# Low-rank log-decay from stacked parts; output projection 2 begins with tokens 0-127; the last gate's sums in two idle stretches

## The reference

```python
mod = jnp.einsum('bd,de->be', silu_c, w_ada[l]) + b_ada[l]
shift1, scale1, gate1, shift2, scale2, gate2 = jnp.split(mod, 6, axis=-1)
h = modulate(rms_norm_2(x, norm1_w[l]), shift1, scale1)
proj = jnp.einsum('btd,de->bte', h, w_in[l])
q, k, v, r, a_lr, su, sv, g_a, g_b = jnp.split(proj, IN_SPLITS, axis=-1)
z = jnp.einsum('btr,rk->btk', a_lr, w_alpha_up[l]) + b_alpha[l]      # rank 16
log_a = jax.nn.log_sigmoid(z.astype(jnp.float32)) / GLA_TAU
o = gla_chunked(q, k, v, log_a)                                     # per head
o_gla = rms_norm_2(o, gla_norm_w[l]) * jax.nn.silu(r)
o_sgu = spatial_gating(gelu(su), gelu(sv), sgu_w[l], sgu_b[l], sgu_ln_w[l], sgu_ln_b[l])
merged = jax.nn.sigmoid(g_a) * o_gla + jax.nn.sigmoid(g_b) * o_sgu
y = jnp.einsum('bte,ed->btd', merged, w_out[l])
x = x + gate1[:, None, :] * y
h2 = modulate(rms_norm_2(x, norm2_w[l]), shift2, scale2)
y2 = peer(h2, peer_w_q[l], peer_keys1[l], peer_keys2[l], peer_down[l], peer_up[l])
x = x + gate2[:, None, :] * y2
```

## Time and profile before

| | us |
|---|---|
| median of 3 runs | 1362.02 |
| lowest, highest | 1361.2, 1363.53 |
| the profiled execution's own time | 1364.04 |
| its span | 1361.8 |
| TensorE busy | 1345.7 |
| GpSimd busy | 1052.1 |
| VectorE busy | 764.7 |
| ScalarE busy | 714.2 |

### The profile page before, as it was taken

One profiled execution on the slowest core, in us unless ns is written; L12 is line 12 of the kernel. 1 busy time (PEld: TensorE's weight loads), 2 busy tenths in 40 slices (PEclk: granted clock), 3 DMA queues, 4 the chain that ended last, 5 costly groups with the idle time before them and its releaser, 6 DMA issues.

```text
span 1361.8 us, 27395 instructions
## 1 busy us (share of the span) xinstructions
PE 1345.7 (99%) x9123; PEld 1176.2 (86%) x9123; DVE 764.7 (56%) x1627; ACT 714.2 (52%) x1145; POOL 1052.1 (77%) x466
## 2 busy tenths in 40 slices
PE   9999999999999999999999999999999999999997
PEld 8798999998788877899999988888888888888886
DVE  4765433336224346289980488888887787411113
ACT  6464655555365445345556544444455555565654
POOL 6665788886787866968888877777777777788885
PEclk9999999998999999999999999999999999999999
DMA  8555677773655455745555545545555454565552
GB/s 311 182 182 189 241 279 283 282 255 110 233 176 183 159 205 211 260 136 180 184 185 185 185 156 170 166 157 169 170 171 170 161 167 164 207 224 191 194 191 102
DMA packets 73056, 263.08 MB, mean 193 GB/s; under 512 B 8224, under 2 KB 9120, under 8 KB 72624
## 3 DMA queue, kind: packets, MB, share of 16 engines
q1 hardware_dynamic: 73008, 262.46, 56.4%
HBM read 259.81 MB, written 2.62 MB: 193 GB/s over the span
## 4 chain that ended last, share of the span: by engine, by line
PE 95%; DVE 3%; ACT 1%; DMA 1%; issue 0%; POOL 0%; SPq 0%; POOLq 0%; DVEq 0%; ACTq 0%
PE bank L1008 15%; PE bank L1010 15%; PE bank L1009 15%; PE bank L989 11%; PE bank L966 8%; PE bank L967 8%; PE bank L968 8%; PE bank L990 5%; PE bank L1486 3%; PE bank L993 2%; PE bank L992 1%; PE bank L1152 1%; PE bank L1468 1%; PE bank L1184 1%; DVE bank L1614 0%; DMA raw<-stream 0%
## 5 line engine op out<-in xcount | busy, mean ns | idle before, releaser
L453 POOL TENSOR_TENSOR wlo<-raw,whi 128x1024 fp32r<-128x1024 f32 x432 | 1037.5, 2413 | 282.5 <-ACT whi L532 281.1
L532 ACT ACTIVATE whi<-raw 128x1024 fp32r<-128x1024 f32 x432 | 456.0, 1057 | 326.9 <-PE bank L1010 257.0
L1008 PE MATMUL bank<-whi,xhl 128*128 128x512 f32 x792 | 314.0, 397 | 1.8 <-DVE xhl L1567 1.6
L1010 PE MATMUL bank<-whi,xhl 128*128 128x512 f32 x792 | 308.9, 390 | 0.0
L1009 PE MATMUL bank<-wlo,xhl 128*128 128x512 f32 x792 | 308.2, 389 | 0.0
L966 PE MATMUL bank<-xhl,whi 128*128 128x256 f32 x896 | 255.0, 285 | 1.9 <-DVE xhl L1572 1.1
L967 PE MATMUL bank<-xhl,whi 128*128 128x256 f32 x896 | 253.5, 283 | 0.0
L968 PE MATMUL bank<-xhl,wlo 128*128 128x256 f32 x896 | 253.4, 283 | 0.0
L989 PE MATMUL bank<-xhl,whi 128*128 128x512 f32 x616 | 222.1, 399 | 0.7 <-DVE xhl L1567 0.7
L1008 PEld LDWEIGHTS bank<-whi,xhl 128*128 128x128 f32 x792 | 148.8, 188 | 34.3 <-DVE xhl L1567 1.9
L966 PEld LDWEIGHTS bank<-xhl,whi 128*128 128x128 f32 x896 | 171.7, 192 | 5.6 <-issue 1.4
(11 more groups left out here) (327 smaller groups left out, 1504.3 us busy)
## 6 DMA issues: line engine op xcount, KB each, us to landing
raw<-stream SPq DMA_DIRECT2D x432, 512.0 KB, 3.3
arena<-ada SPq DMA_DIRECT2D x48, 512.0 KB, 4.7
arena<-rows SPq DMA_DIRECT2D x5, 512.0 KB, 7.6
xs<-x SPq DMA_DIRECT2D x2, 512.0 KB, 6.0
arena<-rows SPq DMA_DIRECT2D x1, 1024.0 KB, 5.9
x_spill<-xs SPq DMA_DIRECT2D x1, 1024.0 KB, 6.6
xs<-x_spill SPq DMA_DIRECT2D x1, 1024.0 KB, 5.5
arena<-hgmask SPq DMA_DIRECT2D x1, 512.0 KB, 8.0
```

The lines of the kernel that those rows point to most:

```text
L453: nc.gpsimd.tensor_tensor(wlo[:, slot, :], raw[:, slot, :], whi[:, slot, :].bitcast(F32), ALU.subtract).then_inc(lo_done, 1)
L532: nc.scalar.activation(whi[:, slot, :], raw[:, slot, :], ACT.Copy).then_inc(hi_done, 1)
L1008: nc.tensor.matmul(bank[b][:, :], ah[:, ts], whi[:, slot, cs], start=start, stop=False)
L1010: last = nc.tensor.matmul(bank[b][:, :], al[:, ts], whi[:, slot, cs], start=False, stop=final)
```

## The change

It has five parts.

1. `ada_columns` of groups 2 to 5 moves 64 columns of ones instead of one; 63 of the 64 results are overwritten or not used.
2. The low-rank product down reads `xhl` directly, in fp32r: ScalarE rounds the 16 weight columns, VectorE puts their rest in 16 more columns beside them, and 8 matmuls with these 32 columns move `xh` and `xl` of a k block together (512 columns). The copies of the modulated rows to the arena (L1970) go, and the product moves from ahead of the group `m_sv` to ahead of its third tile.
3. The low-rank product up stacks three parts on 96 partitions: the weight matrix is sent six times over, and partitions 0-31 hold its upper part, 32-63 the rest, 64-95 the upper part again, against the upper, upper and lower part of the 32 rows from below. Four fp32r matmuls.
4. The transposes of the merged rows go bank by bank, a bank holding four k blocks of 128 tokens. Bank 0's stand ahead of the last product of `m_gb`. Output projection 2 takes k blocks 0 to 2 for tokens 0-127 first, then for tokens 128-255, then k blocks 3 to 5 for all, and the last two bank by bank as before.
5. The last gate's eight tiles have a buffer each, in a dead buffer and in three that are free by then; SP issues them in bursts of 4, 2 and 2 during `m_v` and `m_r`, VectorE sums six of them behind the spatial gating and two behind the second product of the r rows.

The diff, cut (lines of waits and buffers that the text has told are left out):

```diff
@@ buffers
-        mv, mr, mga, mgb, msu, msv = (take(2048, TT, D) for _ in range(6))
+        mv, mr, mga = (take(2048, TT, D) for _ in range(3))
+        spare = take(2048)
+        msu, msv = (take(2048, TT, D) for _ in range(2))
...
+        late_ada = [b_[:, j * 1024:(j + 1) * 1024]
+                    for b_ in (spare, rw.rearrange("p a b -> p (a b)"), qk.rearrange("p a b -> p (a b)"),
+                               msv.rearrange("p a b -> p (a b)")) for j in range(2)]
@@ SyncE
+            sp.wait_ge(S("rw_copied"), 4)
+            for j in range(4):
+                late_ada_tile(j)
+            for n in range(T_IN2_M + 24, T_WOUT2 + 8):
                 tile(n % R, n * P, n - R + 1)
-            for n in range(ADA_FIRST + R, ADA_FIRST + R + 4):
-                ada_tile(n)
+                if n == T_IN2_M + 31:
+                    sp.wait_ge(S("g_qk"), 4)
+                    late_ada_tile(4)
+                    late_ada_tile(5)
+                if n == T_IN2_M + 35:
+                    sp.wait_ge(S("sgu_mm"), 4)
+                    late_ada_tile(6)
+                    late_ada_tile(7)
@@ ScalarE
+            upper_of(T_IN2_F + R + 3, T_IN2_M + 3)
             act.wait_ge(S("consts2_in"), 96)
+            nc.scalar.activation(wal_hl[:, :, 0:16], wal, ACT.Copy)\
+                .then_inc(S("rank_hi"), 1)
+            nc.scalar.activation(wup_hl, wupt, ACT.Copy).then_inc(S("rank_hi"), 1)
...
+            merged_upper(0)
             upper_of(T_WOUT2 + 2, T_WOUT2 + 3)
             act.wait_ge(tile_used, T_IN2_M + 48)
             nc.scalar.activation(bank[3][:, :], bank[3][:, :], ACT.Sigmoid).then_inc(S("gb_out"), 1)
-            upper("merged_T", first=4)
-            upper_of(T_WOUT2 + 3, T_WQ)
+            merged_upper(1)
+            upper_of(T_WOUT2 + 3, T_WOUT2 + 4)
+            merged_upper(2)
+            merged_upper(3)
+            upper_of(T_WOUT2 + 4, T_WQ)
@@ TensorE
-            def ada_columns(g):
+            def ada_columns(g, n=1):
...
-                    last = nc.tensor.matmul(bank[7][:, 4 * g + j:4 * g + j + 1], ada_sum(g)[:, j * P:(j + 1) * P], one,
-                                            start=True, stop=True)
+                    last = nc.tensor.matmul(bank[7][:, 4 * g + j:4 * g + j + n], ada_sum(g)[:, j * P:(j + 1) * P],
+                                            one.to_broadcast([P, n]), start=True, stop=True)
...
-                ada_columns(g)
+                ada_columns(g, 64)
...
+            def low_rank(n):
+
+                if n != 2:
+                    return
+                pe.wait_ge(S("gate1_done"), 2)
+                pe.wait_ge(S("rank_lo"), 1)
+                for k in range(KC):
+                    last = nc.tensor.matmul(bank[6][0:32, :], wal_hl[:, k, :],
+                                            xhl[:, :, k, :], start=(k == 0), stop=(k == KC - 1))
+                last.then_inc(S("alr"), 1)
+
+            m_group(T_IN2_M, "m_sv", before=low_rank)
...
+                    if tt and h == 2:
+                        pe.wait_ge(ada_used, N_ADA)
...
+            def merged_turn_first(b, k):
+                if (b, k) == (3, KC - 1):
+                    merged_turn(0)
...
+            m_group_by_banks(T_IN2_M + 40, "m_gb", 2, ahead=merged_turn_first)
+            merged_turn(1)
+            wout2_part(0, (0, 1))
+            wout2_part(1, (0, 1))
+            merged_turn(2)
+            wout2_part(2, (0, 1))
+            merged_turn(3)
+            for k in range(3):
+                wout2_part(k, (2, 3))
+            for k in range(3, KC - 2):
+                wout2_part(k, range(4))
+            for b in range(4):
+                for k in range(KC - 2, KC):
+                    wout2_part(k, (b,))
@@ VectorE
-            for b in range(4):
-                nc.vector.tensor_copy(xg[:, 2 * b:2 * b + 2, :],
-                                      bank[IN2_BANKS[b]][:, :].rearrange("p (a t) -> p a t", a=2))\
-                    .then_inc(S("xg_out"), 1)
...
+            ttt(wal_hl[:, :, 16:32], wal, wal_hl[:, :, 0:16].bitcast(F32), ALU.subtract).then_inc(S("rank_lo"), 1)
+            ttt(wup_hl[32:64, :], wupt[32:64, :], wup_hl[32:64, :].bitcast(F32), ALU.subtract).then_inc(S("rank_lo"), 1)
             v.wait_ge(S("alr"), 1)
-            nc.vector.tensor_copy(alT, bank[6][0:16, 0:T]).then_inc(S("alr_out"), 1)
+            al = bank[7][0:32, 0:T]
+            own(nc.vector.tensor_reduce(al, bank[6][0:32, :].rearrange("p (a t) -> p t a", a=2), AX.X, ALU.add))
...
+            ttt(al_hl[64:96, :], al, al_hl[0:32, :].bitcast(F32), ALU.subtract)\
+                .then_inc(S("alr_out"), 1)
...
+            v.wait_ge(S("sgu_done"), 4)
+            for n in range(ADA_FIRST, ADA_FIRST + 6):
+                ada_tile(n)
             read_out("m_r", T_IN2_M + 32, mr, "r_out")
...
+            for n in range(ADA_FIRST + 6, N_ADA):
+                ada_tile(n)
             v.wait_ge(S("ga_out"), 4)
...
+            merge(0)
+            merge(1)
+            merged_lower(0)
+            merge(2)
+            merged_lower(1)
+            merge(3)
+            merged_lower(2)
+            merged_lower(3)
```

More of the change, by code:

```diff
@@ L1378, in _ @@
                     ada_row(9)
[L1380 to L1387 removed]
+            def low_rank(n):
[8 more added lines that the diff above has]
+            m_group(T_IN2_M, "m_sv", before=low_rank)
+            pe.wait_ge(S("rank_lo"), 2)
             pe.wait_ge(S("alr_out"), 1)
             for h in range(4):
[L1390 to L1391 removed]
+                last = nc.tensor.matmul(bank[6 + h // 2][:, (h % 2) * T:(h % 2 + 1) * T], wup_hl[:, h * P:(h + 1) * P],
+                                        al_hl, start=True, stop=True)
             last.then_inc(S("z_mm"), 1)
@@ L1432, in _, with merged_turn, wout2_part @@
             last.then_inc(S("gla_o"), 1)
-            m_group_by_banks(T_IN2_M + 40, "m_gb", 2)
-            turn_of("merged_T", go, "merged_out", 0, range(4))
-            turn_of("merged_T", go, "merged_out", 1, (0, 1))
-            def go_turn_rest(k):
-                if k == 1:
-                    turn_of("merged_T", go, "merged_out", 1, (2, 3))
-            m_group_by_banks(T_WOUT2, "wout2", 2, "merged", before=go_turn_rest)
+            def merged_turn(b):
+                pe.wait_ge(S("merged_out"), b + 1)
+                if b == 0:
+                    name, n = acc_freed("merged_T", b)
+                    pe.wait_ge(S(name), n)
+                for j in range(4):
+                    k = 4 * (b % 2) + j
+                    last = nc.tensor.transpose(bank[4 + b][:, j * P:(j + 1) * P], go[:, b // 2, k * P:(k + 1) * P],
+                                               ident[:, :])
+                last.then_inc(acc_ready, 1)
+            def merged_turn_first(b, k):
+                if (b, k) == (3, KC - 1):
+                    merged_turn(0)
+            def wout2_part(k, banks):
+                pe.wait_ge(S("turned_lo"), turn("merged", 4, 2 * (banks[-1] // 2) + k // 4 + 1))
+                m_tile((T_WOUT2 + k) % R, T_WOUT2 + k + 1, xh[:, k, :], xl[:, k, :], "wout2" if k == 0 else None,
+                       final=(k == KC - 1), banks=banks, used=banks[-1] == 3)
+            m_group_by_banks(T_IN2_M + 40, "m_gb", 2, ahead=merged_turn_first)
[12 more added lines that the diff above has]
+                    wout2_part(k, (b,))
             for g in (10, 11):
@@ L1600, in ada_tile @@
                 g, m = n // 4, n % 4
[L1601 to L1603 removed]
+                acc_ = bank[6 if R <= n < ADA_FIRST else 7][:, :]
+                if n < ADA_FIRST:
+                    w_ = adar[:, n % R, :]
+                    v.wait_ge(ada_full[n % R], 16 * (n // R + 1))
+                else:
+                    w_ = late_ada[n - ADA_FIRST]
+                    v.wait_ge(ada_full[(n - ADA_FIRST) // 2], 16 * (ADA_FIRST // R) + 32)
                 if n:
@@ L2094, in _, with merge @@
             v.wait_ge(S("sgu_done"), 4)
-            for b in range(4):
+            def merge(b):
                 tt, cs = b // 2, slice((b % 2) * 512, (b % 2 + 1) * 512)
@@ L2099, in _, with merged_lower @@
                 ttt(go[:, tt, cs], go[:, tt, cs], bank[b][:, :], ALU.add).then_inc(S("merged_out"), 1)
-            turned("merged", None, first=4, banks=(0, 1))
-            v.wait_ge(S("turned_lo"), turn("merged", 4, 1))
-            v.wait_ge(S("gate1_done"), 2)
-            for n in range(ADA_FIRST, ADA_FIRST + 2):
-                ada_tile(n)
-            turned("merged", None, first=4, banks=(2, 3))
-            for n in range(ADA_FIRST + 2, N_ADA):
-                ada_tile(n)
+            def merged_lower(b):
+                tt, ks = b // 2, slice(4 * (b % 2), 4 * (b % 2) + 4)
+                at = slice(tt * P, (tt + 1) * P)
+                v.wait_ge(S("turned_hi"), turn("merged", 4, b + 1))
+                ttt(xl[:, ks, at], bank[4 + b][:, :].rearrange("p (a t) -> p a t", a=4), xh[:, ks, at].bitcast(F32),
```

(3 more changed lines are left out.)

55 lines of the change are left out of this document (26 added, 29 removed).

## The result

Timed side by side on one chip, the changed kernel took 1355.48 us (median of 6 runs, 1354.9 to 1356.16) and the kernel before 1362.62 (median of 6, 1360.83 to 1363.57). The ratio is 0.9945, with a 95% interval of 0.9936 to 0.9955: 7.1 us less by the medians. Forecast were 1354.5 and a range of 1352.3 to 1359.0.

A forecast was written before the change was run, and what follows sets the result against it. TensorE, busy 1345.7 of 1361.8 us, was taken as the bound. Savings of 2.5 + 1.8 + 1.55 + 1.0 + 0.75 = 7.6, taken as 7.5, led from the median 1362.02 to 1354.5 us, range 1352.3 to 1359.0.

The forecast's parts named there:

- The parts' upper bounds: Whole kernel: all parts at their upper bounds give 2 us more than forecast, the range's low end of 1352.3.
- The walk: Step-by-step timing: TensorE ready near 329.6 behind the column sums, saving 2.5; projection 2 starting at 506.1, saving 1.0.
- The rule of the Trainium skill: 16 transposes behind the column groups: not counted as busy, they would lower the clock again and the gain be nothing.
- The fp32 rival: Low-rank products: stacked matmuls run at the fp32 rate, down costs 3.4, up saves 0.2; about 1361, chance 0.05.
- the cover of ScalarE's reading: Behind the low-rank product up: four banks' reading 1.5 us nearer to the next products; counted 0, bound 0.2.
- 0.7 us at most: Ahead of the low-rank product up: VectorE's five operations' longest time each, with five tiles of 2.7 us for them.
- The rival that four switches only move the wait: Start of output projection 2: its wait only moves, 1.75 us less gain, 1356.3; chance 0.12.
- The cover behind L2068: VectorE's 12.77 us idle stretch from 438.3, taking six last-gate tiles (9.3 us): covered by 3.4 us.
- Moving the DMAs: Last gate's bursts between weight tiles: a tile maybe 3.1 us late within 3.6 slack; cost 0, bound 1 us.
- The slower rival: Projection 2's start and transposes before the query projection: clock falls, 3.4 us lost each; two give 1364.1; chance 0.04.

The follow-up runs named there:

- e9: Changed kernel with first halves of two wide tiles taken ahead of their second halves, behind in2 and at the query projection: 1354.49 us, ratio 0.9939.
- e10: Changed kernel with wide tiles' halves in turn at two starts and bank 0's transposes of merged rows one product earlier: 1353.56 us, ratio 0.9931.
- e1: Changed kernel with one column of ones again in the column sums of groups 2 to 5: 1357.83 us, ratio 0.9959.
- e2: Kernel before with only the 64 columns in the column sums: 1360.77 us, ratio 0.9985.
- e3: Kernel before with only the two stacked low-rank products, down and up: 1361.38 us, ratio 0.9983.
- e6: Changed kernel without the keep-warm pairs between the column sums, 64 columns kept: 1356.39 us, ratio 0.9953.
- e7: Changed kernel with ScalarE reading the m_sv banks before its next weight copy: 1355.71 us, ratio 0.9949.
- e4: Changed kernel with the old transposes of merged rows and old start of output projection 2: 1356.60 us, ratio 0.9954.
- e5: Changed kernel with all eight last-gate sums late again, behind the opening of output projection 2, their DMAs still early: 1356.01 us, ratio 0.9951.

## Why the prediction was right

Each of the five parts gained at its place, and the sum was 7.5 against 7.7 by the trace and 7.1 by the medians. The total is closer than the way to it deserves: parts 3 and 5 came out smaller and part 4 larger, and in part 1 two errors cancelled. That is luck. (The parts' upper bounds add up to 2.0 more than the forecast, which gives 1352.5 and not the 1352.3 of the range.) The sizes:

**Part 1, 2.5 forecast, 2.6 by the trace, 2.3 by the medians.** The clock held, the added columns cost nothing, and the transposes are done in their full-clock time. TensorE began the first `f_tile_wide` product at 328.40 (331.99 before: 3.0 earlier, after the start-up) and then stood 0.33 for the lower part of the second four k blocks, which with small losses around it leaves 2.6. The walk had neither: it took TensorE to be ready only near 329.6, 2.5 earlier than before, and had no wait behind that. The second half's transposes were in fact done by 325.7, where the walk let them start at 325.8; the two errors nearly cancel. The place where this part is limited was found afterwards, and e9 and e10 win 0.6 there. The difference between trace and medians was not foreseen: one profiled execution of before showed the fall, and the argument took it for all. The times and mean clocks of e1, e2 and e3 show that it comes in some. The trace of before was one of the slower executions (1364.04 against a median of 1362.62), so a sum made against it overstates what the median gains. The prediction knew that this execution was 2 us slower than the median and still subtracted its whole sum from the median; that this did little harm is due to the 0.4 that part 4 gave beyond its forecast, which is luck too.

The rule of the Trainium skill, "TensorE: Matmul & The Clock Gate", Part 4, that transposes don't count as busy, speaks against this part. Here the 16 transposes ran, in 2.1 us, and the clock stayed at 1.00 throughout. The stronger evidence against the rule is the trace of before, where the clock rose at 329.5 while TensorE had done nothing but transposes since 326.3. Two other traces leave it open: in e3 the clock stayed at 0.50 through all 16 transposes (to 328.4) and rose at 330.0, behind the row product, and in e6 it fell at 325.6, behind 1.5 us of waiting and eight transposes. So what the runs show is that this part gained, not how transposes count.

**Part 2, 1.8 forecast, 1.9 measured.** 1.85 for the eight products, as L989's rate said, and no loss behind them (0.23 for the next product, against 0.43). The fp32 rival is out.

**Part 3, 1.55 forecast, 1.3 measured.** This is the term that was mis-sized, by the cover of ScalarE's reading. The four products take 0.47, as forecast (0.48). But the next group's first product writes a bank that ScalarE must read first, and ScalarE's timeline in the changed kernel shows a weight copy and an activation table load ahead of that reading,

```profile
374.41 1.06 ACT L548 ACTIVATE whi<-raw 128x1024 fp32r<-128x1024 f32 x1 [1.66 <-PE bank L1040]
375.49 1.28 ACT L797 ACT_TABLE_LOAD   x1
376.79 0.60 ACT L797 ACTIVATE arena<-bank 128x512 f32<-128x512 f32 x1
```

so bank 0 has been read at 377.4, just when the low-rank products end (377.5), where before they ended 1.5 us behind that point. The next product starts at 377.62 and its piece of the chain is 0.47 instead of 0.23. The prediction had seen this cover, counted 0 and gave 0.2 as a bound; it had the bank read about 0.1 ahead of its need, as it came, but not that a product starts only some time behind such a reading, here 0.23. e7 makes the reading earlier and gets 0.27. The operations of VectorE for it took longer than "0.7 us at most", but stood early enough:

```profile
354.03 1.41 DVE L2045 TENSOR_TENSOR ul<-arena,ul 128x128 fp32r<-128x128 f32 x1
355.47 2.77 DVE L2046 TENSOR_TENSOR uh<-arena,uh 32x512 fp32r<-32x512 f32 x1
```

**Part 4, 1.0 forecast, 1.4 by the trace, 1.1 by e4.** The chain of the changed kernel:

```profile
497.76 0.45 PE bank L1478 x4
498.24 0.61 ACT xhl L874
498.87 0.70 DVE xhl L2183
499.62 0.50 PE bank L1038
...
502.63 0.44 PE bank L1478 x4
503.07 0.24 PE bank L1038
```

The start at 499.6 is the forecast 506.1 less the 6.3 gained by then and 0.1 more. What the walk had too large were the transposes between products (0.44 for four, where it took 0.54 from a row of eight in a block) and a wait for bank 3's merge, which did not come. The rival that four switches only move the wait is out: TensorE waits there once, for 0.3, and e4, without this part, has the 1.6 back.

**Part 5, 0.75 forecast, 0.55 by the trace, 0.5 by e5.** VectorE is free when the first bank is ready,

```profile
518.57 0.70 DVE L2196 TENSOR_TENSOR bank<-bank,arena 128x512 f32<-128x512 f32 x1 [12.31 <-PE bank L1040]
...
523.99 0.75 DVE L2202 TENSOR_SCALAR arena<-xs,st 128x1024 f32<-128x1024 f32 x1
```

and needs 5.4 us for four banks, 1.36 each, the pace of TensorE; the last pair then stands 1.5 us behind TensorE's last product, not 1.3, and TensorE still waits 0.5 where 0.3 was forecast. The cover behind L2068 of the old kernel was estimated to shrink to 3.4 us and shrank to 2.9:

```profile
439.40 2.41 DVE L1681 SCALAR_TENSOR_TENSOR bank<-arena,st,bank 128x512 f32<-128x512 f32 x3
444.75 2.73 DVE L2062 COPY arena<-bank 128x512 f32<-128x512 f32 x4 [2.94 <-PE bank L1040]
```

Moving the DMAs was forecast to cost nothing, and cost nothing: TensorE waits for no other engine between 378 and 499 us. It was closer than it looks. Behind the first burst ScalarE stood 1.28 us for a weight tile, and GpSimd had that tile's lower part done at 418.9 us, 2.3 us before its use at 421.2.

What the sum of parts left out is that the parts don't stand alone. One by one in the kernel before, e2 and e3 each lost 0.6 to 0.7 us of their gain at the wait before the query projection (medians 2.3 and 1.7). In the changed kernel nothing is lost there, since VectorE's sums no longer stand between a DMA and the residual. So part 5 should be worth more than its own 0.5 of e5, whose DMAs were early: it keeps what parts 1 to 3 gave. How much more is not shown, because no run has the other four parts with sums and DMAs both late.

**The slower rival** (clock falls in the openings) did not come: its place, the start of output projection 2, has a granted clock of 1.00 (seventh figure), with TensorE busy for 4.71 of 5 us and then throughout:

```profile
495.00:500.00 5.00, 4.71 (x26) 3.74 (x25) 3.82 (x6) 2.92 (x5) 3.19 (x3) 1.00 0.69 234
500.00:505.00 5.00, 5.00 (x28) 4.14 (x27) 3.46 (x6) 2.39 (x5) 4.63 (x2) 1.00 0.43 166
```

## What to carry to other kernels

A stretch in which TensorE streams a single column at a time can lose the clock in some executions and keep it in others; widen such matmuls, keep the full-size ones between them (e6), and compare several runs with their mean clocks, since one trace shows one of the two. When a change shortens the bound engine's work, look at what reads the bank it writes next: the cover may have been worth a few tenths. A burst of DMAs that starts only when buffers come free, with a chain of another engine's work behind it, can take back part of the gains ahead of it (here 0.6 to 0.7 us of 2.7 and of 3.2), so move that first or together. And where a pass over several weight tiles waits for the second half of its input, take the first halves of two tiles ahead: that gave 0.6 us at each of two places here.

## What was not expected of the hardware

- With one-column groups the clock falls only in some executions of the same kernel: 3 of 5 runs of e1 by their times and mean clocks (0.996 and 0.997 for 0.998 and 0.999), and two groups of times in e3, whose medians are 2.5 us apart.
- Four fp32 matmuls of 64 columns cost hardly more than four of one: 0.84 us for 0.79, and with the keep-warm pair behind them 1.36 for 1.37.
- An fp32 transpose between products takes 0.11 us (0.44 for four), in a block of eight 0.136.
- VectorE's operations with two inputs from the on-chip memory (SBUF) and GpSimd's weight tiles hold each other up. In the changed kernel the same instruction on the same shape took 1.28 us when it began ahead of GpSimd's tile and 2.75 when it began within it, and that tile, which began within the first of the two, took 3.26 for the usual 2.40:

```profile
330.76 1.28 DVE L2021 SCALAR_TENSOR_TENSOR xs<-xs,st,arena 128x1024 f32<-128x1024 f32 x1
...
332.63 2.75 DVE L2021 SCALAR_TENSOR_TENSOR xs<-xs,st,arena 128x1024 f32<-128x1024 f32 x1
```

```profile
331.03 3.26 POOL L469 TENSOR_TENSOR wlo<-raw,whi 128x1024 fp32r<-128x1024 f32 x1 [5.79 <-ACT whi L548]
...
352.89 2.40 POOL L469 TENSOR_TENSOR wlo<-raw,whi 128x1024 fp32r<-128x1024 f32 x1
```

  The subtraction of 128x128 from the arena, begun at 354.03, ended at 355.44 (1.41 us), just behind the second of these tiles (355.29). The one of 32x512 (2.77 us) ended at 358.24, behind a tile that ended at 357.70. One that reads a bank and has 128x512 takes 0.69. The Trainium skill, "SBUF — State Buffer", section "SBUF: two separate sides", says that a VectorE operation with two SBUF inputs and a GpSimd operation that reads SBUF exclude each other for a whole instruction, whichever starts first. The trace agrees, by these ends and durations.
